# Differential attention inside a two-block network on one core: v panels three heads later, stages spaced by panels, the score bias added by TensorE

## The chip, the core and the metric

One core of a Trainium2 chip runs the whole forward pass of two blocks as one program. The metric is the device time of one execution in microseconds (us); the kernel before takes 2347.14 us (median of three runs, 2345.76 to 2347.51).

The core's engines run their own instruction queues in order and meet only at semaphores: TensorE (PE, matmuls and transposes into the eight banks of PSUM), VectorE (DVE), ScalarE (ACT), GpSimd (POOL) and SyncE (SP, which issues the weight loads).

## What is computed

Two blocks with thirteen phases: feed-forward layers, two hybrid mixers, one differential attention, one retention layer. The change is in the differential attention (phase `da`), 8 heads over 256 positions, head width 128 made of two halves of 64:

```python
def _diff_attention(xn, w_in, q_gain, k_gain, lam, subln, w_out, lam_init):
    q, k, v = jnp.split(xn @ w_in, 3, axis=-1)
    q = _rms(q.reshape(B, T, H, 2, Dh), q_gain) * (Dh ** -0.5)
    k = _rms(k.reshape(B, T, H, 2, Dh), k_gain)
    ...
    slopes = 2.0 ** (-8.0 * jnp.arange(1, H + 1, dtype=jnp.float32) / H)
    ...
        s = jnp.einsum('bhmqd,bhmkd->bhmqk', qb, k, preferred_element_type=jnp.float32)
        dist = (q_pos[:, None] - key_pos[None, :]).astype(jnp.float32)
        bias = jnp.where(dist >= 0, -slopes[:, None, None] * dist, -jnp.inf)
        p = jax.nn.softmax(s + bias[None, :, None], axis=-1)
        a = p[:, :, 0] - lmbda * p[:, :, 1]
        return jnp.einsum('bhqk,bhkd->bhqd', a.astype(v.dtype), v)
    ...
    o = _rms(o, subln) * (1.0 - lam_init)
    return o.reshape(B, T, H * 2 * Dh).astype(xn.dtype) @ w_out
```

## The kernel before

**Weights.** Every weight matrix is cut into panels of 128 output columns, [128, 1024] in float32. SP loads a panel into one of four slots of `raw` (`RING` is 4). ACT rounds it into `whi` (`act_split`, L318), DVE subtracts to get the rest `wlo` (`dve_split`, L325), and PE multiplies in three products per block of 128 rows (`products`, L308 to L310): 24 matmuls of 256 columns for one panel. The hi and lo parts of panel j+4 use the slot of panel j: ACT's split waits until PE has used panel j (`panel_used`), and DVE's waits for ACT's (`hi_ready`).

**The phase `da`** has 24 input panels, in the order q, k, v of head 0, q, k, v of head 1, and so on, then 8 output panels. A panel's result stands in bank 0 or 1, in turn, and DVE reads it out (`read_out`, L1342) times the row factor `R`; PE may start panel j when panel j-2 is read out (`a_evac`). Right behind each read-out, DVE makes the `wlo` of panel j+4.

**A head's stages** run one or more iterations of t behind its panels. With the line numbers of the profile: squares of q and k on ACT (`dsq`, L1041), their sums by a float32 matmul on PE (L683), the factor (`drq`, L402 and L404, ACT), q and k normed (`dn`, L1366, DVE), split into `dn_hi` (L1034, ACT) and `dn_lo` (L1389, DVE), scores (L723, PE, banks 6 and 7), bias (`dsc`, L1401), maxima (L1405, L1406) and their negation (L1408) on DVE, exponentials from `dsc` with their sums (`dp`, L1016, ACT), the weights `da_` (L1373 to L1383, DVE), their transposes (L733, PE), split into `dT_hi` (L1044, ACT) and `dT_lo` (L1411, DVE), v transposed (L701, PE) and split into `dv_hi` (L1025, ACT) and `dv_lo` (L1361, DVE), weighted values (L693, PE), a copy `do_` (L1357, DVE), its squares `dosq` (L1031, ACT), their sums (L740, PE), the factor `dro` (L402, L404, ACT), the normed output `don` (L1416, DVE), and its parts `dy_hi` (L1007, ACT) and `dy_lo` (L1347, DVE).

**What sets the order.** All of it is written out by hand, one loop over t for each engine; nothing is rescheduled. Each engine takes its queue strictly in that order, so an instruction that waits holds everything written behind it. When the input panels are through, PE fills in matmuls of the first four output panels (`out_tiles`) between the last heads' stages. The split of output panel 28 can't start before panel 24 has been used, so it comes after the last head.

## Time and profile before

| | us |
|---|---|
| median of three runs | 2347.14 |
| profiled execution, its own time | 2347.09 |
| its span on the core | 2345.3 |
| PE / DVE / ACT / POOL busy in the span | 2284.2 / 1484.6 / 1199.8 / 280.6 |
| phase `da`, first input panel to the next phase's first panel | 148.7 |
| granted TensorE clock over the span | 0.985 of full |

The page gives busy time by engine and by line. A matmul's record lasts longer than the spacing of two matmuls, so that a busy PE in the page is an engine with work in flight; where it loses time is read from its waits and from the timeline. The chain of waits follows the work that ended last back through the engines, and shows which engine's queue sets the pace of a stretch.

### The profile page before, as it was taken

Reading aid. Unit: us, or ns where it says so; the run is one execution under the profiler, and the core shown is the slowest. Engines: PE = TensorE matmul, PEld = TensorE weight load, DVE = VectorE, ACT = ScalarE, POOL = GpSimd, SP = SyncE. Lnnn points to the kernel's source line nnn. Section 1 sums busy time; section 2 is a strip of 40 time slices with the busy share of each in tenths; the row PEclk is TensorE's granted clock in tenths of the full one; section 3 lists DMA queues with packets and bytes.
Section 4 is the critical chain, followed back from the end, with each engine's and each line's share of the span. In section 5 each row is a group of like instructions: output and inputs, shape, how many; then the busy total and the mean of one; then the engine's idle time right before and its main releaser. Section 6 shows DMA issues by size and latency. Waiting matters only on the chain.

```text
span 2345.3 us, 48880 instructions
## 1 busy us (share of the span) xinstructions
PE 2284.2 (97%) x18478; PEld 2267.1 (97%) x18478; DVE 1484.6 (63%) x2284; ACT 1199.8 (51%) x1723; POOL 280.6 (12%) x328
## 2 busy tenths in 40 slices
PE   7999999999999999899998999889999999999999
PEld 7999999999999999899998999789999999999999
DVE  6655786665566468676656656866646655675663
ACT  5444675544444357654545545654535544464552
POOL 2001460300100125220010010020010010001000
PEclk9999999999999999899999999989999999999999
DMA  6555433555455553255554554325655555445563
GB/s 206 170 194 163 146 101 105 171 179 182 159 179 183 169 168 127 73 180 186 199 168 158 191 191 147 126 91 182 206 167 181 195 180 173 144 154 179 188 205 126
DMA packets 100881, 386.52 MB, mean 165 GB/s; under 512 B 11280, under 2 KB 13456, under 8 KB 100784
## 3 DMA queue, kind: packets, MB, share of 16 engines
q1 hardware_dynamic: 100128, 383.89, 49.8%
q8 instruction: 63, 1.03, 0.2%
q0 software_dynamic: 368, 1.20, 0.1%
q14 instruction: 34, 0.28, 0.0%
q10 hardware_dynamic: 288, 0.12, 0.0%
HBM read 384.11 MB, written 1.05 MB: 164 GB/s over the span
## 4 chain that ended last, share of the span: by engine, by line
PE 89%; DVE 6%; ACT 3%; issue 1%; POOL 0%; DMA 0%; ACTq 0%; POOLq 0%; DVEq 0%
PE bank L308 28%; PE bank L310 28%; PE bank L309 28%; DVE wlo L325 2%; ACT whi L318 1%; PE bank L540 1%; PE bank L669 1%; PE bank L570 1%; PE bank L795 0%; DVE qk L1237 0%; PE bank L583 0%; ACT dp L1016 0%; DVE dsc L1401 0%; DVE bank L1223 0%; PE bank L805 0%
## 5 line engine op out<-in xcount | busy, mean ns | idle before, releaser
L308 PE MATMUL bank<-u_hi,whi 128*128 128x256 f32 (+1 forms) x3968 | 1140.8, 287 | 20.2 <-DVE wlo L325 20.2
L310 PE MATMUL bank<-u_hi,wlo 128*128 128x256 f32 (+1 forms) x3968 | 1134.0, 286 | 0.0
L309 PE MATMUL bank<-u_lo,whi 128*128 128x256 f32 (+1 forms) x3968 | 1132.5, 285 | 0.0
L325 DVE TENSOR_TENSOR wlo<-raw,whi 128x1024 fp32r<-128x1024 f32 (+1 forms) x680 | 884.7, 1303 | 209.2 <-ACT whi L318 207.5
L318 ACT ACTIVATE whi<-raw 128x1024 fp32r<-128x1024 f32 (+1 forms) x680 | 746.5, 1111 | 286.6 <-PE bank L310 284.0
L308 PEld LDWEIGHTS bank<-u_hi,whi 128*128 128x128 f32 x3968 | 755.8, 190 | 21.5 <-DVE wlo L325 15.2
L310 PEld LDWEIGHTS bank<-u_hi,wlo 128*128 128x128 f32 x3968 | 755.8, 190 | 0.0
L309 PEld LDWEIGHTS bank<-u_lo,whi 128*128 128x128 f32 x3968 | 753.5, 190 | 0.7
L310 PE MATMUL bank<-hid_hi,wlo 128*128 128x256 f32 (+1 forms) x1408 | 400.6, 285 | 0.0
L308 PE MATMUL bank<-hid_hi,whi 128*128 128x256 f32 (+1 forms) x1408 | 399.4, 284 | 0.0
L309 PE MATMUL bank<-hid_lo,whi 128*128 128x256 f32 (+1 forms) x1408 | 398.1, 283 | 0.0
L1171 DVE TENSOR_TENSOR up<-bank,R 128x256 f32<-128x256 f32 (+1 forms) x176 | 75.7, 430 | 336.9 <-PE bank L310 336.9
L308 PEld LDWEIGHTS bank<-hid_hi,whi 128*128 128x128 f32 x1408 | 265.4, 188 | 0.0
L309 PEld LDWEIGHTS bank<-hid_lo,whi 128*128 128x128 f32 x1408 | 265.1, 188 | 0.0
L310 PEld LDWEIGHTS bank<-hid_hi,wlo 128*128 128x128 f32 x1408 | 264.7, 188 | 0.0
L339 ACT ACTIVATE u_hi<-h,gain 128x256 fp32r<-128x256 f32 (+1 forms) x88 | 44.6, 512 | 288.0 <-DVE h L1151 282.1
L365 POOL TENSOR_TENSOR ssq<-h 128x256 f32<-128x256 f32 (+1 forms) x12 | 10.4, 865 | 1353.0 <-DVE h L1151 1347.9
L861 ACT ACTIVATE sl<-gt 128x256 f32<-128x256 f32 (+1 forms) x160 | 67.7, 423 | 195.6 <-DVE gt L1169 195.5
L1151 DVE SCALAR_TENSOR_TENSOR h<-bank,h 128x256 f32<-128x256 f32 (+1 forms) x96 | 41.2, 429 | 194.2 <-PE bank L310 192.5
L865 ACT ACTIVATE hid_hi<-pr 128x256 f32 (+1 forms) x160 | 67.8, 424 | 154.7 <-DVE pr L1175 154.7
L1558 POOL TENSOR_TENSOR proj<-proj,tprod 128x272 f32<-128x272 f32 (+1 forms) x120 | 115.8, 989 | 88.0 <-ACT tprod L899 88.0
L370 POOL TENSOR_TENSOR sq<-h 128x256 f32<-128x256 f32 (+1 forms) x84 | 56.0, 666 | 366.5 <-DVE h L1151 364.5
(233 smaller groups left out, 2094.3 us busy)
## 6 DMA issues: line engine op xcount, KB each, us to landing
raw<-w SPq DMA_DIRECT2D x552, 512.0 KB, 3.3
raw<-w SPq DMA_DIRECT2D x128, 704.0 KB, 4.4
proj<-xT SPq DMA_DIRECT2D x2, 544.0 KB, 4.8
outT<-h SPq DMA_DIRECT2D x8, 128.0 KB, 4.6
consts<-cst POOLq DMA_DIRECT2D x1, 512.0 KB, 4.7
dist<-cst POOLq DMA_DIRECT2D x1, 192.0 KB, 2.7
rdist<-cst POOLq DMA_DIRECT2D x1, 192.0 KB, 2.7
sgain<-small POOLq DMA_DIRECT2D x1, 145.5 KB, 4.8
```

Of the source, the lines that this page charges most:

```text
L308: pe.matmul(out, w_h, x_hi, start=first, stop=False)
L309: pe.matmul(out, w_h, x_lo, start=False, stop=False)
L310: return pe.matmul(out, w_l, x_hi, start=False, stop=last)
L318: act.activation(whi[:, n % RING, 0:COLS[n]], raw[:, n % RING, 0:COLS[n]], ACT.Copy).then_inc(hi_ready, 1)
L325: dve.tensor_tensor(wlo[:, n % RING, 0:COLS[n]], raw[:, n % RING, 0:COLS[n]], whi[:, n % RING, 0:COLS[n]], ALU.subtract).then_inc(lo_ready, 1)
L339: act.activation(u_hi[:, f, win(y)], h[:, f, win(y)], ACT.Copy, scale=norm_gain(y, f)).then_inc(u_hi_ready, 1)
L370: pool.tensor_tensor(sq[:, win(y)], h[:, f, win(y)], h[:, f, win(y)], ALU.mult).then_inc(sq_done, 1)
L861: act.activation(sl[:, p, W], gt[:, p, W], ACT.Silu).then_inc(silu_done, 1)
L865: act.activation(hid_hi[:, f, W], pr[:, p, W], ACT.Copy).then_inc(hid_hi_ready, 1)
L1151: dve.scalar_tensor_tensor(out=h[:, f, W], in0=src, scalar=factor, in1=h[:, f, W], op0=ALU.mult, op1=ALU.add).then_inc(h_done, 1)
L1171: dve.tensor_tensor(up[:, p, W], bank[(g + 1) % 4][:, 0:N], R[:, W], ALU.mult).then_inc(a_evac, 1)
L1558: pool.tensor_tensor(acc, acc, tprod[:, (i - first) % TAP_RING, W2], ALU.add)\
```

## The change

- The input panels of `da` come in another order (`DA_PANELS`): iteration t brings q and k of head t and v of head t-3. The last three iterations' v panels stand behind q and k of head 7.
- A head's stages move: scores(t-2), transposes of the weights (t-3) and of v (t-4) stand behind the q panel, weighted values (t-4) behind the k panel, the q and k sums of head t and the output sums of head t-4 behind the v panel. ACT's and DVE's queues are reordered with them, and the tail is written out stage by stage on all three.
- The bias is added on PE: two matmuls of 384 columns for each head, `slope_r` (the identity times the slope) by `dist_r`. GpSimd makes both once (9 instructions). The 12 score matmuls alternate between the halves of the array instead of taking them one after the other.
- `dsc` is gone: DVE takes the maxima from banks 6 and 7, negated in the same instruction, and ACT's exponentials read the banks.
- The transposed weights have a bank of their own (5) and `dT_hi` and `dT_lo` two buffers; the output sums go to the second half of bank 3.

```diff
+V_LAG = 3
+DA_PANELS = [(part, t - (V_LAG if part == 2 else 0)) for t in range(DA_HEADS + V_LAG) for part in range(3)]
+DA_PANELS = [(part, hd) for part, hd in DA_PANELS if 0 <= hd < DA_HEADS]
...
+            dist_r = sb("dist_r", [128, 384], f32r, area)
+            slope_r = sb("slope_r", [128, DA_HEADS, 128], f32r, area)
...
-            dsc = sb("dsc", [128, 2, 384], f32, area)
...
+        bank = [ctx.enter_context(nc.psum_tensor(f"bank{i}", [128, 512], f32)) for i in range(6)]
+        pair67 = ctx.enter_context(nc.psum_tensor("bank67", [128, 2, 512], f32))
+        bank += [pair67[:, 0, :], pair67[:, 1, :]]
...
+                def qk_sums(hd):
+                    pe.wait_ge(d_sq_done, 2 * (hd + 1))
+                    pe.matmul(bank[4][:, :], mean_64, dsq[:, :, :].rearrange("p a t -> p (a t)"),
+                              start=True, stop=True).then_inc(d_qksum, 1)
+                def scores(hd):
+                    pe.wait_ge(d_n_ready, hd + 1)
+                    if hd == 0:
+                        pe.wait_ge(d_bias_ready, DA_HEADS + 1)
+                    else:
+                        pe.wait_ge(d_exps, 4 * hd)
+                    for i, (c0, w) in enumerate(((0, 128), (128, 256))):
+                        for n, (qq, kk) in enumerate(((dn_hi, dn_hi), (dn_hi, dn_lo), (dn_lo, dn_hi))):
+                            for m in range(2):
+                                rows = slice(64 * m, 64 * m + 64)
+                                pe.matmul(bank[6 + m][:, c0:c0 + w],
+                                          qq[rows, 0, 128 * i:128 * i + 128], kk[rows, 1, 0:w],
+                                          start=(i == 0 and n == 0), stop=False, skip_group_check=True)
+                    for m in range(2):
+                        mm = pe.matmul(bank[6 + m][:, 0:384], slope_r[:, hd, :], dist_r[:, :],
+                                       start=False, stop=True, skip_group_check=True)
+                    mm.then_inc(d_s_full, 1)
...
+                for t in range(DA_HEADS):
+                    in_panel2(y, DA_PANELS.index((0, t)))
                     if t == 0:
                         pe_norm(pe, y)
+                    if t >= 2:
+                        scores(t - 2)
                     if t >= 3:
+                        transpose_a(t - 3)
+                    if t >= 4:
+                        transpose_v(t - 4)
+                    if 1 <= t <= V_LAG:
+                        qk_sums(t - 1)
+                    in_panel2(y, DA_PANELS.index((1, t)))
+                    if t >= 4:
+                        weighted_values(t - 4)
+                    if t >= V_LAG:
+                        in_panel2(y, DA_PANELS.index((2, t - V_LAG)))
+                        qk_sums(t)
+                    if t >= 4:
+                        out_sums(t - 4)
+                in_panel2(y, DA_PANELS.index((2, 5)))
+                scores(6)
+                transpose_a(5)
+                transpose_v(4)
+                in_panel2(y, DA_PANELS.index((2, 6)))
+                weighted_values(4)
+                transpose_v(5)
+                in_panel2(y, DA_PANELS.index((2, 7)))
+                out_sums(4)
+                scores(7)
+                transpose_a(6)
+                transpose_v(6)
+                weighted_values(5)
+                out_tiles(0, 2, 0, 4)
+                out_sums(5)
+                transpose_v(7)
+                weighted_values(6)
+                out_tiles(2, RING, 0, 4)
+                out_sums(6)
+                transpose_a(7)
+                out_tiles(0, RING, 4, 6)
+                weighted_values(7)
+                out_tiles(0, RING, 6, 7)
+                out_sums(7)
...
+                def exps(hd):
+                    act.wait_ge(d_nmax, 2 * (hd + 1))
+                    for i, (c0, w) in enumerate(((0, 128), (128, 256))):
+                        for m in range(2):
+                            j = 2 * i + m
+                            act.activation(dp[:, m, c0:c0 + w], bank[6 + m][:, c0:c0 + w], ACT.Exp,
+                                           bias=dst[:, 4 + j:5 + j], accum_out=dst[:, 8 + j:9 + j])\
+                               .then_inc(d_exps, 1)
...
+                for t in range(DA_HEADS):
+                    if t >= 5:
+                        out_factor(t - 5)
+                    split(0, t)
                     if t >= 4:
+                        v_high(t - 4)
+                    if t >= 1:
+                        qk_factor(t - 1)
                     if t >= 3:
+                        weights_high(t - 3)
+                    if t >= 5:
+                        normed_hi(t - 5)
+                    if t >= 2:
+                        exps(t - 2)
+                    if t >= 1:
+                        qk_high(t - 1)
+                    split(1, t)
+                    if t >= 4:
+                        out_squares(t - 4)
+                    qk_squares(t)
+                    if t >= V_LAG:
+                        split(2, t - V_LAG)
...
+                def row_max(hd):
+                    dve.wait_ge(d_s_full, hd + 1)
+                    dve.tensor_reduce(dst[:, 4:6], pair67[:, :, 0:128], AX.X, ALU.max, negate=True).then_inc(d_nmax, 1)
+                    dve.tensor_reduce(dst[:, 6:8], pair67[:, :, 128:384], AX.X, ALU.max, negate=True).then_inc(d_nmax, 1)
...
-                            dve.scalar_tensor_tensor(out=dsc[:, m, :], in0=dist[:, :], scalar=-slopes[hd],
-                                                     in1=bank[6 + m][:, 0:384], op0=ALU.mult,
-                                                     op1=ALU.add).then_inc(d_sc_done, 1)
...
-                        dve.tensor_scalar(dst[:, 4:8], dst[:, 0:4], -1.0, None, ALU.mult).then_inc(d_nmax, 1)
...
+                for t in range(DA_HEADS):
+                    panel(0, t)
                     if t >= 4:
+                        v_low(t - 4)
+                    if t >= 2:
+                        row_max(t - 2)
+                    if t >= 5:
+                        normed(t - 5)
+                    if t >= 1:
+                        qk_normed(t - 1)
+                    panel(1, t)
                     if t >= 3:
+                        weights_low(t - 3)
+                    if t >= 4:
+                        out_copy(t - 4)
+                    if t >= 1:
+                        qk_low(t - 1)
+                    if t >= 5:
+                        normed_lo(t - 5)
+                    if t >= 2:
+                        weights(t - 2)
+                    if t >= V_LAG:
+                        panel(2, t - V_LAG)
...
+                    for hd in range(DA_HEADS):
+                        pool.tensor_scalar(slope_r[:, hd, :], ident, -2.0 ** (-8.0 * (hd + 1) / DA_HEADS), None,
+                                           ALU.mult).then_inc(d_bias_ready, 1)
+                    pool.wait_ge(table_loaded, 16)
+                    pool.tensor_copy(dist_r[:, :], dist[:, :]).then_inc(d_bias_ready, 1)
...
+            p8.append(w[[part * DA_HEADS + hd for part, hd in DA_PANELS]])
```

Lines of the changed kernel in the excerpts below: L317 to L319 panel matmuls, L327 `whi`, L334 `wlo`, L1445 read-out.

TensorE before, in iteration 5, from the output sums to the second panel (`d_osq` is the semaphore of `dosq`, `d_sq_done` of `dsq`):

```order
L740 MATMUL bank<-dosq,consts 128x256 [waits d_osq]
L308 MATMUL bank<-u_hi,whi 128x256 [waits a_evac,lo_ready]
...
L683 MATMUL bank<-dsq,consts 128x512 [waits d_sq_done]
L693 MATMUL bank<-dT_hi,dv_hi 128x256 [waits d_o_done,d_T_ready]
...
L701 MATMUL bank<-consts,dv 128x128 [waits a_evac]
...
L308 MATMUL bank<-u_hi,whi 128x256 [waits a_evac,lo_ready]
```

TensorE with the change, the same engine from the k panel's end in one iteration to the scores of the next:

```order
L737 MATMUL bank<-dT_hi,dv_hi 128x256 [waits d_ro_done,d_v_ready,d_T_ready]
...
L317 MATMUL bank<-u_hi,whi 128x256 [waits a_evac,lo_ready]
...
L687 MATMUL bank<-dsq,consts 128x512 [waits d_sq_done]
L745 MATMUL bank<-dosq,consts 128x256 [waits d_osq]
L317 MATMUL bank<-u_hi,whi 128x256 [waits a_evac,lo_ready]
...
L701 MATMUL bank<-dn_hi 128x128 [waits d_exps,d_n_ready]
```

The sums of q and k of head t now stand in the iteration that makes these panels, one panel behind k, where they stood a panel into the next iteration, two panels behind k.

ScalarE before, from the exponentials of one head to the squares of q and k:

```order
L1016 ACTIVATE dp,dst<-dsc,dst 128x256 x2
L1007 ACTIVATE dy_hi<-don 128x256 [waits d_on_done]
L318 ACTIVATE whi<-raw 128x1024 [waits panel_used,raw_loaded3]
L1025 ACTIVATE dv_hi<-bank 128x256 [waits d_vt_full]
L402 ACTIVATE drq<-bank,epsilons 128x512 [waits d_qksum]
L404 ACTIVATE drq<-drq 128x512 [waits d_rq_log]
L1031 ACTIVATE dosq<-do_ 128x256 [waits d_o_done]
L1034 ACTIVATE dn_hi<-dn 128x512 [waits d_n_done]
L318 ACTIVATE whi<-raw 128x1024 [waits panel_used,raw_loaded0]
L318 ACTIVATE whi<-raw 128x1024 [waits panel_used,raw_loaded1]
L1041 ACTIVATE dsq<-dqk 128x256 [waits a_evac]
```

ScalarE with the change, from the transposed weights to the squares of q and k in iteration 5:

```order
L1074 ACTIVATE dT_hi<-bank 128x384 [waits d_t_full]
L1057 ACTIVATE dy_hi<-don 128x256 [waits d_on_done]
L1081 ACTIVATE dp,dst<-bank,dst 128x128 [waits d_nmax]
L1081 ACTIVATE dp,dst<-bank,dst 128x128
L1081 ACTIVATE dp,dst<-bank,dst 128x256 x2
L1089 ACTIVATE dn_hi<-dn 128x512 [waits d_s_full,d_n_done]
L327 ACTIVATE whi<-raw 128x1024 [waits panel_used,raw_loaded1]
L1098 ACTIVATE dosq<-do_ 128x256 [waits d_o_done]
L1094 ACTIVATE dsq<-dqk 128x256 [waits a_evac]
L1094 ACTIVATE dsq<-dqk 128x256
L327 ACTIVATE whi<-raw 128x1024 [waits panel_used,raw_loaded2]
```

The squares `dosq` of another head's output moved to the place right ahead of `dsq`, and both stand behind the exponentials and the k panel's split.

VectorE with the change, in the same iteration, from the q panel's split to the copy `do_`:

```order
L334 TENSOR_TENSOR wlo<-raw,whi 128x1024 [waits hi_ready]
L1467 TENSOR_TENSOR dv_lo<-bank,dv_hi 128x256 [waits d_v_hi]
L1472 TENSOR_REDUCE dst<-bank 128x2 [waits d_s_full]
L1473 TENSOR_REDUCE dst<-bank 128x2
L1462 SCALAR_TENSOR_TENSOR don<-do_,lam,dro 128x256 [waits d_y_ready,d_ro_done]
L1478 SCALAR_TENSOR_TENSOR dn<-dqk,lam,drq 128x256 [waits d_rq_done]
L1478 SCALAR_TENSOR_TENSOR dn<-dqk,sgain,drq 128x256
L1445 TENSOR_TENSOR dqk<-bank,R 128x256 [waits panel_used]
L334 TENSOR_TENSOR wlo<-raw,whi 128x1024 [waits hi_ready]
L1506 TENSOR_TENSOR dT_lo<-bank,dT_hi 128x384 [waits d_T_hi]
L1514 COPY do_<-bank 128x256 [waits d_on_done,d_osq,d_av_full]
```

The maxima moved from behind two panels' read-outs and splits to between the q and the k panel; the copy `do_` stands behind the k panel's split.

## Rows read from the trace of the kernel before

**Rows 1.** The page, busy us of each engine, share of the span, instructions

```profile
PE 2284.2 (97%) x18478; PEld 2267.1 (97%) x18478; DVE 1484.6 (63%) x2284; ACT 1199.8 (51%) x1723; POOL 280.6 (12%) x328
```

**Rows 2.** Busy time in stretches of `da`: its iterations 0 to 3, one later, tail

```profile
core 0: us, PE busy (x) PEld busy (x) DVE busy (x) ACT busy (x) POOL busy (x), PEclk, DMA share, GB/s
1420.60:1479.60 59.00, 56.07 (x454) 52.17 (x452) 45.54 (x89) 39.78 (x79) 2.05 (x3) 1.00 0.43 140
1479.60:1493.10 13.50, 12.35 (x102) 11.37 (x100) 11.36 (x26) 9.58 (x23) 0.00 (x0) 1.00 0.37 117
...
1520.10:1551.90 31.80, 22.83 (x132) 20.02 (x130) 16.22 (x41) 13.42 (x38) 0.00 (x0) 0.77 0.11 34
```

**Rows 3.** Chain of waits in one iteration of `da`: start us, us, what

```profile
1480.66 0.94 DVE dsc L1401 x2
...
1482.04 0.60 DVE dst L1406
...
1482.88 0.87 ACT dp L1016 x4
...
1484.74 0.31 ACT dy_hi L1007
1485.05 0.96 ACT whi L318
...
1486.03 1.22 DVE wlo L325
...
1487.59 0.33 DVE do_ L1357
```

**Rows 4.** Timeline of DVE and ACT in that iteration: start us, us, what

```profile
1482.75 0.55 DVE L1411 TENSOR_TENSOR dT_lo<-bank,dT_hi 128x384 fp32r<-128x384 f32 x1
1483.22 0.47 DVE L1416 SCALAR_TENSOR_TENSOR don<-do_,lam,dro 128x256 f32<-128x256 f32 x1
...
1478.10 0.72 ACT L1041 ACTIVATE dsq<-dqk 128x256 f32<-128x256 f32 x2
...
1487.96 0.42 ACT L1031 ACTIVATE dosq<-do_ 128x256 f32<-128x256 f32 x1 [0.46 <-DVE do_ L1357]
1489.08 0.63 ACT L1034 ACTIVATE dn_hi<-dn 128x512 fp32r<-128x512 f32 x1 [0.70 <-DVE dn L1366]
```

**Rows 5.** Groups by line and form in that iteration: busy us, mean ns

```profile
L1007 ACT ACTIVATE dy_hi<-don 128x256 fp32r<-128x256 f32 x1 | 0.4, 400 | 0.0
...
L1025 ACT ACTIVATE dv_hi<-bank 128x256 fp32r<-128x256 f32 x1 | 0.4, 361 | 0.0
```

**Rows 6.** Timeline: PE from sums to transposes, a panel's end, a wait before scores

```profile
1432.39 1.02 PE L683 MATMUL bank<-dsq,consts 128*128 128x512 f32 x2
1433.25 0.38 PE L701 MATMUL bank<-consts,dv 128*128 128x128 f32 x2
...
1439.03 0.28 PE L310 MATMUL bank<-u_hi,wlo 128*128 128x256 f32 x1
...
1439.40 1.06 ACT L318 ACTIVATE whi<-raw 128x1024 fp32r<-128x1024 f32 x1 [1.58 <-PE bank L310]
...
1451.41 0.33 PE L723 MATMUL bank<-dn_hi 64*128 64x128 f32 x1 [1.15 <-DVE dn_lo L1389]
```

**Rows 7.** PE's waits over the whole run: us in total, times, longest

```profile
PE bank L540 <- ACT at_hi L974: 9.1, 5, 2.3
...
PE bank L693 <- DVE dT_lo L1411: 4.6, 3, 2.6
PE bank L669 <- DVE dy_lo L1347: 4.2, 2, 2.4
```

**Rows 8.** Timeline of PE: two of its waits, idle us in brackets

```profile
992.52 0.39 PE L308 MATMUL bank<-qk,whi 128*128 128x256 f32 x1 [1.56 <-DVE proj L1312]
...
1523.87 0.58 PE L693 MATMUL bank<-dT_hi,dv_hi 128*128 128x256 f32 x1 [2.56 <-DVE dT_lo L1411]
```

**Rows 9.** Busy time right behind one of the mixer's waits, columns as in rows 2

```profile
352.90:359.60 6.70, 6.70 (x31) 6.68 (x31) 0.78 (x2) 2.03 (x4) 1.73 (x2) 0.50 0.01 2
```

More of the change, by code:

```diff
@@ new lines, in weighted_values @@
+                def weighted_values(hd):
+                    pe.wait_ge(d_T_ready, hd + 1)
+                    pe.wait_ge(d_v_ready, hd + 1)
+                    if hd >= 1:
+                        pe.wait_ge(d_ro_done, hd)
+                    for i, (c0, t0) in enumerate(((0, 0), (256, 128))):
+                        for n, (vv, aa) in enumerate(((dv_hi, dT_hi), (dv_hi, dT_lo), (dv_lo, dT_hi))):
+                            mm = pe.matmul(bank[3][:, t0:SEQ], vv[:, hd % 2, 128 * i:128 * i + 128],
+                                           aa[:, hd % 2, c0:c0 + SEQ - t0], start=(i == 0 and n == 0),
+                                           stop=(i == 1 and n == 2), skip_group_check=True)
+                    mm.then_inc(d_av_full, 1)
@@ L685, in da @@
                     if t >= 3:
-                        hd = t - 3
-                        pe.wait_ge(d_T_ready, hd + 1)
-                        if hd >= 1:
-                            pe.wait_ge(d_o_done, hd)
-                        for i, (c0, t0) in enumerate(((0, 0), (256, 128))):
-                            for n, (vv, aa) in enumerate(((dv_hi, dT_hi), (dv_hi, dT_lo), (dv_lo, dT_hi))):
-                                mm = pe.matmul(bank[3][:, t0:SEQ], vv[:, hd % 2, 128 * i:128 * i + 128],
-                                               aa[:, c0:c0 + SEQ - t0], start=(i == 0 and n == 0),
-                                               stop=(i == 1 and n == 2), skip_group_check=True)
@@ new lines, in qk_high, with qk_squares @@
+                def qk_high(hd):
+                    act.wait_ge(d_n_done, 2 * (hd + 1))
+                    if hd >= 1:
+                        act.wait_ge(d_s_full, hd)
+                    act.activation(dn_hi[:, :, :], dn[:, :, :], ACT.Copy).then_inc(d_n_hi, 1)
+                def qk_squares(hd):
+                    act.wait_ge(a_evac, A + DA_PANELS.index((1, hd)) + 1)
+                    for i in range(2):
+                        act.activation(dsq[:, i, :], dqk[:, hd % 2, i, :], ACT.Square).then_inc(d_sq_done, 1)
@@ new lines, in panel, with normed @@
+                def panel(part, hd):
+                    if part == 2 and hd >= 1:
+                        dve.wait_ge(d_vt_full, hd)
+                    read_out(DA_PANELS.index((part, hd)), dv[:, :] if part == 2 else dqk[:, hd % 2, part, :])
+                def normed(hd):
+                    dve.wait_ge(d_ro_done, hd + 1)
+                    if hd >= 1:
+                        dve.wait_ge(d_y_ready, hd)
+                    dve.scalar_tensor_tensor(out=don[:, :], in0=do_[:, :], scalar=sub_gain, in1=dro[:, :],
+                                             op0=ALU.mult, op1=ALU.mult).then_inc(d_on_done, 1)
@@ new lines, in da @@
+                qk_normed(7)
+                normed(3)
+                panel(2, 5)
+                v_low(4)
+                row_max(6)
+                weights_low(5)
+                qk_low(7)
+                normed_lo(3)
+                out_copy(4)
+                weights(6)
+                panel(2, 6)
+                v_low(5)
+                normed(4)
+                row_max(7)
+                weights_low(6)
+                normed_lo(4)
+                panel(2, 7)
+                v_low(6)
```

273 lines of the change are left out of this document (121 added, 152 removed).

## The prediction

> **What bounds the kernel now.** I read the page first. It calls TensorE 97% busy [rows 1], but this counts records that overlap. The table by stretches comes next: in each later iteration of phase `da` (13.5 us) DVE is busy 11.4, ACT 9.6 and PE 12.4, at full clock; the tail of 31.8 us has PE busy 22.8 and a granted clock of 0.77 [rows 2]. In such an iteration PE waits 1.15 us ahead of the scores, for DVE [rows 6]. So PE's own work is 13.5 - 1.2 = 12.3 us per head, and something else makes 13.5.
>
> The chain of waits says what [rows 3]. It runs on DVE all the time but for one piece: maxima, then ACT's four exponentials (from 1482.88 to the next instruction at 1484.74), `dy_hi` 0.31, the split `whi` 0.96, and back to DVE's `wlo` 1.22. DVE needs that split before it may go on. A loop over two in-order queues sets the pace: 10.3 us of DVE and 3.2 of ACT, 13.5 in all.
>
> **The change, part by part.**
>
> *DVE's work per head.* `dsc` goes (0.94 [rows 3]), and the negation with it, about 0.2. The maxima stay at 0.34 + 0.60 [rows 3]. That they read PSUM costs nothing by the rows, and ACT gains: it takes `dv_hi` out of PSUM in 361 ns and `dy_hi` out of SBUF in 400 [rows 5], so four exponentials save 0.1 to 0.2. The Trainium skill (Perfetto Trace Analysis, Optimizing Scalar/DVE Operations) gives DVE a higher fixed cost on PSUM than on SBUF, some 65 ns more, and ACT a lower one, some 42 ns less; ACT's rows agree. By the page the pair is worth 2 x 0.065 - 4 x 0.042, nothing, per head.
>
> *PE's work per head.* Two bias matmuls of 384 columns. The trace has none; between the panel's spacing of 0.119 for 256 columns (2.86 a panel) and 0.43 for one pass of a 512-column float32 sum (half of 1432.39 to 1433.25 [rows 6]) I take 0.17 each, near the first, 0.33 a head, range 0.24 to 0.86. The alternating scores give some back, 0 to 0.4. PE stays at about 12.2 a head; this is not on the chain below.
>
> *GpSimd's nine instructions* have fifteen us until the first scores. They cost nothing; without that cover a few us, once.
>
> *The order.* This is the main term. I follow the new queues through iteration t (5 to 7), with the lengths from the rows, each as start to next start:
> 1. PE's q panel, start to last matmul 2.8, then 0.37 until ACT's split starts (1439.03 to 1439.40 [rows 6]): 3.2.
> 2. `whi` of the q slot 1.0 to 1.1, DVE's `wlo` 1.15, `dv_lo` 0.33: 2.5 [rows 3].
> 3. Maxima 0.94, `don` 0.47 [rows 3, 4], which now stands right behind them: 1.4.
> 4. ACT: `dy_hi` 0.31, exponentials 1.7, `dn_hi` 0.54 [rows 3, 4]: 2.6.
> 5. `whi` of the k slot 1.1, `wlo` 1.15: 2.25.
> 6. DVE's `dT_lo` 0.47 and copy `do_` 0.42 + 0.03 [rows 3, 4]: 0.9.
> 7. ACT's `dosq` 0.33, then `dsq` twice 0.72 [rows 4]: 1.1.
> 8. PE's q and k sums 0.82 [rows 6], output sums 0.25: 1.1. Behind them is the q panel of t+1.
>
> Sum 15.05; I take 15.0. Each link is either the next instruction of an in-order queue or a semaphore. The loop before held one split pair with the exponentials between; this one holds two splits, the exponentials, the copy with two squares and one PE panel. PE arrives at the sums 12.2 us after it left them, so it **waits 2.8 us per head there**, where it waited 1.2 before the scores. Queued behind the waiting sums are the output sums and the q panel, and the whole chain waits for that panel. Iteration 4 has no `don` and `dy_hi` yet, 14.2.
>
> The same way for the rest. *Iterations 0 to 3* make only 9 of the 24 panels: 9 x 2.86 + four q and k sums 3.3 + two sets of scores 2.4 + the norm and one transpose 0.6 = 32.0, and 1.7 of waits for DVE's `dn_lo` and weights: 33.7. *Iterations 4 to 7*: 14.2 + 3 x 15.0 = 59.2. *Tail*, three v panels among it: from the v panel of head 5, DVE and ACT alternate through q/k norm (6.6), maxima to exponentials of head 6 (2.9), exponentials to `dn_lo` (2.9), weights and a read-out (4.4), maxima to `dT_hi` and `dy_hi` (3.9), a read-out, split, `dv_lo`, copy and square (3.1): 23.8. Then PE work of 11.0 to the last sums, the last normalisation 2.8, and 12 matmuls 1.4: 39.0. Sum 33.7 + 59.2 + 39.0 = 131.9.
>
> Before it is 59.0 + 3 x 13.5 + 31.8 + 1.4 = 132.7 [rows 2], of which about 5 are due to the half clock in the tail. From here on both kernels have the same four output panels. So at full clock the change comes out 0.8 us shorter than the row of before, and 4 longer than before would be at full clock.
>
> *The clock* decides the rest. In the trace every PE wait of 1.8 us or more stands beside a stretch at 0.5: the four of about 2.2 in the mixers, those of 2.56 and 1.91 for `dT_lo`, those of 1.80 and 2.44 for `dy_lo` [rows 7, 8]. The one of 1.56 [rows 8] and the 1.15s do not. Behind one of 2.2 the clock is at 0.5, its 1.2 GHz level, for 6.7 us, and 31 matmuls take the time that 56 would at 0.119 [rows 9]: 3.0 us lost. The new waits are 2.0 (iteration 4) and 2.8 (5, 6, 7), and what follows each is on the chain: 1.1 of sums and a panel, 4 us of PE work, so the loss lands in full. Bounds 0 to 4 x 3.0; I take three of four, 9.0. The tail still has two long waits (ahead of output sums 3.4, of the last matmuls 2.6): 2.5. Together 11.5.
>
> Forecast: 2347.1 - 0.8 + 11.5 = **2357.8 us**. The profiled run's 2347.09 is its span and 1.8, and equals the median.
>
> **Rivals.**
> - *The clock stays up.* Waits of 2.8 every 15 us leave long work between. Then only the tail's 2.5 is left: 2347.1 - 0.8 + 2.5 = 2348.8, no change that can be told. For it: in iterations of 15 us with 12.2 of matmuls PE is busier than in the mixers. Against: eight of eight in the rows. The Trainium skill (TensorE: Matmul & The Clock Gate, Why this matters for your kernels) warns only of idle gaps longer than any of these, which is this rival's case; the rows speak against that rule. Chance 0.10.
> - *Some waits only*: one or two at 3.0, 2351.8 to 2355. Chance 0.17.
> - *The other side, faster.* The chain decides only if ACT reaches `dsq` later than PE reaches the sums. If its links overlap by more than 2.8 us, PE's 12.2 sets the pace: 4 x 2.8 less, no half clock in the middle: 2348.8 - 10.4 = 2338.4. For it: DVE's and ACT's work per head is down to 10.2 and 9.1. Against: the same reading gives 13.5 for before, which is the measured period. Chance 0.13.
> - *The change misses its cover further*: all four waits, a third one in the tail, the maxima slower on PSUM across two banks: 2362 to 2368. Chance 0.10.
> - The forecast's own case, 2355 to 2362: 0.50.
>
> **How the numbers follow.** The range reaches from 2346, which takes in the rival with the clock up, to 2366; what is left out is the faster case and the end of the slow one, under 0.2. A measurement of this kernel can tell 0.2%, 4.7 us, from no change. Slower by more (over 2351.8): 0.50 + 0.10 + 0.13 of the third case = 0.73. Within: 0.10 + 0.04 = 0.14. Faster (under 2342.4): 0.13.
>
> **What the profile of the changed kernel would show.** Iterations 5 to 7 of `da` with a period of 15 or, with half clock, 18 us; PE's longest wait in the phase ahead of the q and k sums, put down to ACT's `dsq`, 2.0 to 2.9 each, and none of 1 us ahead of the scores; a granted clock under 1 in the middle of the phase, where it is 1.00 now; a chain of waits that goes panel, `whi`, `wlo`, maxima, `don`, `dy_hi`, exponentials, `whi`, `wlo`, copy, squares, sums. Wrong: a period near 12.3 and PE unbroken; or a period of 15 at full clock, which would make the clock step wrong; or scores with bias over 2 us.

## The result

The changed kernel takes **2355.26 us** (median of 7, 2354.32 to 2357.07), the kernel before it, measured beside it, 2347.85 (7, 2345.76 to 2349.14). The ratio is 1.0031, with a 95% interval of 1.002 to 1.0042: slower by 0.3%. The forecast was 2357.8 in a range of 2346 to 2366, with 0.73 on slower. The profiled execution took 2355.55 us, its span is 2353.8.

One number is used for all kernels below. The phases ahead of `da` are the same code in all of them, but in the profiled executions they end anywhere from 1417.4 to 1421.2, so I compare the time **from the first matmul of `da` to the end of the span**: 924.7 before (first matmul at 1420.64 of 2345.3) and 933.4 after (1420.42 of 2353.8). The change costs 8.7 us there. Each of these numbers is from one profiled execution, and a stretch of 3.4 us at half clock (a granted clock of 0.50) more or less moves it by up to 1.7.

### The profile page after: what moved, and what is told of

Its sections match the earlier page's. It is cut to its first block, busy times and chain, and to the rows that moved or that the text cites. A ratio compares the mean times of both kernels' runs of the same rounds, so it can differ in the third digit from the quotient of the medians.

```text
span 2353.8 us, 48939 instructions
## 1 busy us (share of the span) xinstructions
PE 2287.5 (97%) x18494; PEld 2269.5 (96%) x18494; DVE 1476.9 (63%) x2260; ACT 1197.7 (51%) x1723; POOL 287.2 (12%) x337
## 4 chain that ended last, share of the span: by engine, by line
PE 89%; DVE 5%; ACT 4%; issue 1%; POOL 0%; DMA 0%; ACTq 0%; DVEq 0%; POOLq 0%
PE bank L317 28%; PE bank L319 28%; PE bank L318 28%; DVE wlo L334 2%; ACT whi L327 1%; PE bank L549 1%; PE bank L579 1%; ACT dp L1081 0%; PE bank L845 0%; DVE qk L1341 0%; PE bank L592 0%; PE bank L678 0%; DVE u_lo L355 0%; PE bank L687 0%; DVE bank L1327 0%
## 5 line engine op out<-in xcount | busy, mean ns | idle before, releaser
L317 PE MATMUL bank<-u_hi,whi 128*128 128x256 f32 (+1 forms) x3968 | 1146.2, 289 | 20.2 <-DVE wlo L334 20.1
L319 PE MATMUL bank<-u_hi,wlo 128*128 128x256 f32 (+1 forms) x3968 | 1136.9, 287 | 0.0
L334 DVE TENSOR_TENSOR wlo<-raw,whi 128x1024 fp32r<-128x1024 f32 (+1 forms) x680 | 886.2, 1305 | 210.5 <-ACT whi L327 208.6
L327 ACT ACTIVATE whi<-raw 128x1024 fp32r<-128x1024 f32 (+1 forms) x680 | 747.4, 1112 | 296.6 <-PE bank L319 294.4
L317 PEld LDWEIGHTS bank<-u_hi,whi 128*128 128x128 f32 x3968 | 758.8, 191 | 22.5 <-DVE wlo L334 15.0
L319 PEld LDWEIGHTS bank<-u_hi,wlo 128*128 128x128 f32 x3968 | 758.5, 191 | 0.0
L319 PE MATMUL bank<-hid_hi,wlo 128*128 128x256 f32 (+1 forms) x1408 | 401.1, 285 | 0.0
L317 PE MATMUL bank<-hid_hi,whi 128*128 128x256 f32 (+1 forms) x1408 | 399.9, 284 | 0.0
L317 PEld LDWEIGHTS bank<-hid_hi,whi 128*128 128x128 f32 x1408 | 265.7, 189 | 0.0
L319 PEld LDWEIGHTS bank<-hid_hi,wlo 128*128 128x128 f32 x1408 | 265.1, 188 | 0.0
```

The costliest lines, as they stand in the source:

```text
L317: pe.matmul(out, w_h, x_hi, start=first, stop=False)
L319: return pe.matmul(out, w_l, x_hi, start=False, stop=last)
L327: act.activation(whi[:, n % RING, 0:COLS[n]], raw[:, n % RING, 0:COLS[n]], ACT.Copy).then_inc(hi_ready, 1)
L334: dve.tensor_tensor(wlo[:, n % RING, 0:COLS[n]], raw[:, n % RING, 0:COLS[n]], whi[:, n % RING, 0:COLS[n]], ALU.subtract).then_inc(lo_ready, 1)
```

## The profile after

The page's busy line of the changed kernel answers to [rows 1]:

```profile
PE 2287.5 (97%) x18494; PEld 2269.5 (96%) x18494; DVE 1476.9 (63%) x2260; ACT 1197.7 (51%) x1723; POOL 287.2 (12%) x337
```

DVE lost 24 instructions and 7.7 us, TensorE has 16 matmuls and 3.3 us, GpSimd 9 instructions and 6.6 us more. This line alone does not say where the 8.7 us come from.

Busy time in stretches of `da` of the changed kernel, columns as in [rows 2]: iterations 0 to 3; iteration 6; then two pieces, one behind the third of four waits and one behind the fourth; and, from another answer, the tail, from its first v panel to the last output matmul:

```profile
1420.42:1454.15 33.73, 32.55 (x260) 29.75 (x258) 23.35 (x39) 24.63 (x49) 9.21 (x12) 1.00 0.47 150
1485.95:1502.68 16.73, 14.16 (x103) 13.05 (x102) 10.38 (x23) 9.39 (x22) 0.00 (x0) 0.90 0.30 93
...
1502.90:1506.20 3.30, 3.30 (x17) 3.30 (x16) 1.46 (x2) 0.89 (x2) 0.00 (x0) 0.50 0.17 43
1519.60:1523.00 3.40, 3.40 (x34) 3.24 (x32) 1.56 (x3) 1.12 (x3) 0.00 (x0) 1.00 0.17 37
```
```profile
1519.48:1562.85 43.37, 34.11 (x247) 31.20 (x245) 22.39 (x51) 20.12 (x51) 0.61 (x1) 0.90 0.15 49
```

Read the second row against the 13.50 of [rows 2]: DVE is busy a full microsecond less, and the iteration is 3.2 us longer. 2.57 of the 16.73 are idle PE, and the granted clock is 0.90, where it was 1.00.

PE's waits in `da` after (us in total, times, longest), to be read beside [rows 7]:

```profile
PE bank L687 <- ACT dsq L1094: 9.7, 4, 2.6
PE bank L745 <- ACT dosq L1098: 4.1, 2, 3.0
PE bank L678 <- DVE dy_lo L1450: 2.4, 1, 2.4
...
PE bank L701 <- DVE dn_lo L1484: 1.1, 2, 0.7
```

The wait ahead of the scores (1.15 an iteration in [rows 6]) is gone; in its place PE waits four times, 9.7 us together, ahead of the q and k sums (line 687), for ACT's squares. The timeline of PE shows the first of them and the third:

```profile
1467.82 0.70 PE L687 MATMUL bank<-dsq,consts 128*128 128x512 f32 x1 [1.95 <-ACT dsq L1094]
...
1501.48 1.13 PE L687 MATMUL bank<-dsq,consts 128*128 128x512 f32 x2 [2.57 <-ACT dsq L1094]
1502.44 0.66 PE L745 MATMUL bank<-dosq,consts 128*128 128x256 f32 x2
1502.68 0.63 PE L317 MATMUL bank<-u_hi,whi 128*128 128x256 f32 x1
```

The chain of waits through iteration 6 (start us, us, what), to be read beside [rows 3]. The panel's matmuls between the first row and `whi` are left out:

```profile
1486.51 0.21 PE bank L317
...
1490.70 1.07 ACT whi L327
...
1491.79 1.23 DVE wlo L334
...
1493.38 0.41 DVE dst L1472
1493.79 0.60 DVE dst L1473
1494.39 0.40 DVE don L1462
...
1494.82 0.05 ACT dy_hi L1057
...
1496.84 0.52 ACT dn_hi L1089
1497.36 0.95 ACT whi L327
...
1499.48 0.55 DVE dT_lo L1506
1500.03 0.34 DVE do_ L1514
...
1500.40 0.03 ACT dosq L1098
...
1500.72 0.71 ACT dsq L1094 x2
...
1501.48 1.13 PE bank L687 x2
1502.61 0.49 PE bank L745 x2
```

These are the eight links of the prediction in their order. The lengths, start to next start: panel 4.75 (1485.95 to 1490.70; predicted 3.2), `whi`, `wlo`, `dv_lo` 2.68 (2.5), maxima and `don` 1.44 (1.4), `dy_hi`, exponentials, `dn_hi` 2.54 (2.6), the second split pair 2.12 (2.25), `dT_lo` and copy 0.92 (0.9), squares 1.08 (1.1), sums 1.20 (1.1). Together 16.73. Only the panel is far off, by 1.55, and it is off because many of its matmuls stand 0.21 apart, at half clock; the other seven are within 0.2 each.

## The experiments

Before a chip ran any of them two theories stood. **The loop**: PE waits because the q and k sums close a loop over three in-order queues, 15 us long, and the clock adds to it. **PE's own work**: the two bias matmuls, or something else on PE, make the time. e5 to e8 were thought out after the first four had run. The table gives the time, its ratio to the kernel before with the 95% interval, and the time from the first matmul of `da` to the end; the last is from one profiled execution. The kernel before was timed again beside each set: 2347.9 belongs to e1 to e4, 2346.4 to e5 to e8, and the changed kernel has the 2347.85 of the result. Each ratio is to the one beside it.

| kernel | us | ratio | from `da` |
|---|---|---|---|
| before | 2347.9 and 2346.4 (two sets) | 1 | 924.7 |
| changed | 2355.3 | 1.0031 (1.0020 to 1.0042) | 933.4 |
| e1: old order, bias on PE | 2336.1 | 0.9955 (0.9941 to 0.9968) | 913.5 |
| e2: changed, sums later | 2340.9 | 0.9972 (0.9963 to 0.9982) | 917.4 |
| e3: changed, matmuls in the wait | 2351.4 | 1.0016 (1.0007 to 1.0025) | 927.6 |
| e4: changed, bias on DVE | 2370.5 | 1.0096 (1.0080 to 1.0111) | 948.3 |
| e5: e1, scores alternating | 2334.3 | 0.9950 (0.9937 to 0.9964) | 911.6 |
| e6: changed, `dsq` first | 2344.9 | 0.9994 (0.9985 to 1.0004) | 922.7 |
| e7: changed, matmuls behind the wait | 2361.7 | 1.0067 (1.0052 to 1.0082) | 939.6 |
| e8: e5, sums earlier in the tail | 2331.6 | 0.9939 (0.9926 to 0.9953) | 910.4 |

### e1: the bias on TensorE alone, in the old order

> The order of panels and stages is that of the kernel before; only the bias goes to TensorE, the maxima and exponentials read PSUM. Loop theory: the 13.5 us loop of before loses dsc (0.94), the negation (0.2) and some of the exponentials (0.1), so that TensorE's own 12.3 us per head sets the pace; no new wait over 1.8 us in the iterations, granted clock 1.00 there. Median 2337 to 2341, against 2347.9 for before. Rival (the bias on TensorE or reading PSUM is what made the change slower): 2348 to 2356.

The kernel before, with nothing of the new order. In PE's `scores`, in ACT's exponentials and in DVE's maxima:

```diff
+                        for m in range(2):
+                            mm = pe.matmul(bank[6 + m][:, 0:384], slope_r[:, hd, :], dist_r[:, :],
+                                           start=False, stop=True, skip_group_check=True)
...
-                                act.activation(dp[:, m, c0:c0 + w], dsc[:, m, c0:c0 + w], ACT.Exp,
+                                act.activation(dp[:, m, c0:c0 + w], bank[6 + m][:, c0:c0 + w], ACT.Exp,
...
-                            dve.scalar_tensor_tensor(out=dsc[:, m, :], in0=dist[:, :], scalar=-slopes[hd],
...
+                        dve.tensor_reduce(dst[:, 4:6], pair67[:, :, 0:128], AX.X, ALU.max, negate=True).then_inc(d_nmax, 1)
+                        dve.tensor_reduce(dst[:, 6:8], pair67[:, :, 128:384], AX.X, ALU.max, negate=True).then_inc(d_nmax, 1)
```

It is 0.45% faster than before, just under the lower end of what I expected. One iteration of e1, same columns as above, and its PE timeline from the scores on:

```profile
1464.70:1477.40 12.70, 12.70 (x103) 11.86 (x102) 10.47 (x22) 9.49 (x23) 0.00 (x0) 1.00 0.38 129
```
```profile
1472.20 0.33 PE L728 MATMUL bank<-dn_hi 64*128 64x128 f32 x1
...
1473.37 0.62 PE L733 MATMUL bank<-dist_r,slope_r 128*128 128x384 f32 x2
1473.83 0.49 PE L741 MATMUL bank<-consts,da_ 128*128 128x128 f32 x3
```

PE is busy for all of 12.70: the DVE-ACT loop of 13.5 is now shorter than PE's own work, and there is no wait in an iteration. The scores with bias take 1.63 us (1472.20 to 1473.83), where those of before take 1.17, so the two bias matmuls cost 0.46, not 0.33, and inside the range of 0.24 to 0.86. The change holds a part that gains 11 us; whatever loses is in the order. Only 4.3 of the 11 lie ahead of the output sums of iteration 7 (99.2 us from the first matmul of `da` before, 94.9 in e1). The other 6.8 lie behind, where before has stretches of 6.8, 3.4 and 13.7 us at half clock and e1 has none.

### e5: and the scores alternate

> The order of the kernel before, with the bias on TensorE and maxima and exponentials from PSUM, as e1, and in addition the twelve score matmuls alternate between the two halves. In e1 the period of an iteration was 12.7 us and PE waited for nothing of 0.9 us or more in it, so PE sets the pace there. In the kernel before and in e1 the twelve take some 1.17 us, in the changed kernel and in e4 some 0.86. Theory (the pace is PE's own work): the period falls by the 0.3 us that the alternation saves, to 12.4, and eight heads give 2.4 us: 2333 to 2335. Rival (DVE-ACT loop is just as long as PE's work by now, so that a shorter PE only waits): period stays 12.7, 2336, and PE gets waits of 0.3 us ahead of the scores.

```diff
-                        for m in range(2):
-                            rows = slice(64 * m, 64 * m + 64)
-                            for i, (c0, w) in enumerate(((0, 128), (128, 256))):
-                                for n, (qq, kk) in enumerate(((dn_hi, dn_hi), (dn_hi, dn_lo), (dn_lo, dn_hi))):
+                        for i, (c0, w) in enumerate(((0, 128), (128, 256))):
+                            for n, (qq, kk) in enumerate(((dn_hi, dn_hi), (dn_hi, dn_lo), (dn_lo, dn_hi))):
+                                for m in range(2):
+                                    rows = slice(64 * m, 64 * m + 64)
```

The same rows of e5:

```profile
1467.30:1479.75 12.45, 12.45 (x103) 11.61 (x102) 10.38 (x22) 9.48 (x23) 0.00 (x0) 1.00 0.39 128
```
```profile
1474.82 0.33 PE L728 MATMUL bank<-dn_hi 64*128 64x128 f32 x2
...
1475.70 0.62 PE L733 MATMUL bank<-dist_r,slope_r 128*128 128x384 f32 x2
1476.16 0.49 PE L741 MATMUL bank<-consts,da_ 128*128 128x128 f32 x3
```

The block is 1.34 (1474.82 to 1476.16) and the period 12.4; PE stays unbroken, as the theory wanted and the rival did not. From `da` on that is 2.0 us less. The two ratios overlap, so it is the traces that show this gain, not the times alone; neither trace has a stretch at half clock in the phase. Against e5 the order of the changed kernel costs 933.4 - 911.6 = **21.8 us**, of which some 8.5 are half clock by the estimates of the part on the prediction (4.8 in the iterations, 3.7 in the tail).

### e2: the sums later in the new order

> The change, with one edit: the sums of q and k and of the outputs stand behind the next q panel on TensorE instead of ahead of it (and the output factor behind the q panel's split on ScalarE). Loop theory: the panel no longer waits for the squares, the loop of 15 us is cut, the period falls to 12.3 us, the three waits of 2.6 us and their stretches at half clock go: 2341 to 2345. Rival (the three heads' delay of v, or the work itself, costs the time): 2353 to 2357.

```diff
                     if t == 0:
                         pe_norm(pe, y)
+                    if t >= 5:
+                        out_sums(t - 5)
+                    if t >= 4:
+                        qk_sums(t - 1)
                     if t >= 2:
                         scores(t - 2)
...
                         in_panel2(y, DA_PANELS.index((2, t - V_LAG)))
-                        qk_sums(t)
-                    if t >= 4:
-                        out_sums(t - 4)
```

ACT's `out_factor` moves behind `split(0, t)` to match. The q panel of t+1 is no longer queued behind the waiting sums. One iteration of e2:

```profile
1469.60:1482.00 12.40, 12.40 (x103) 11.42 (x102) 9.27 (x20) 8.72 (x22) 0.00 (x0) 1.00 0.39 117
```

The period is 12.4 for 16.7, with no wait and no half clock in it; from `da` on it takes 16.0 us less than the changed kernel, some of it because its tail has 6.8 us at half clock where that one's has 13.7. Its median of 2340.9 is just under the 2341 to 2345 expected. What it still loses to e5, 5.8 us, must be outside these iterations, which are as long as e5's. Over the whole phase (140.8 us, e5's is 134.9) PE is idle 2.5 us more and busy 3.4 us more. Two stretches of 3.4 us at half clock in e2's tail, where e5 has none, account for about 3.0 of the busy time (half of the 3.2 and 2.9 that PE is busy in them).

### e6: one step of ACT turned round

> The changed kernel with one step of ACT's order turned round: the squares of q and k (dsq) stand ahead of the square of the output (dosq), so they don't wait for DVE's dT_lo and copy do_. Theory (the loop of eight links that the prediction gives is what sets 15 us): without the 0.9 us of dT_lo and copy and the 0.33 of dosq ahead of dsq the period of iterations 5 to 7 falls from 15.2 to about 13.5 to 14; what is left of the wait is at the output sums, about 1 us for dosq, and the waits at the q and k sums are under 0.5. Waits that short bring no stretch at a clock of 0.5 in the iterations. Together 5.8 plus 3 x 1.5: 2345 to 2350. Rival (PE's wait is owed to something outside the loop, so that it only moves behind the q and k sums in full): period stays 15, 2355.

```diff
+                    qk_squares(t)
                     if t >= 4:
                         out_squares(t - 4)
-                    qk_squares(t)
```

One iteration of e6, and its wait for a square (us in total, times, longest):

```profile
1478.40:1492.20 13.80, 12.96 (x101) 11.57 (x101) 10.47 (x23) 9.29 (x22) 0.00 (x0) 1.00 0.35 114
```
```profile
PE bank L745 <- ACT dosq L1098: 6.9, 6, 3.0
```

Two calls in another order give 10.7 us back (933.4 to 922.7), and with 0.9994 the kernel can't be told from before. The period is 13.8 where the links said 13.5 to 14; the waits ahead of `dsq` are gone from the list, what is left is for `dosq`, under a microsecond an iteration, and no stretch of the iterations is at half clock. The copy `do_` and `dT_lo` were links of the loop: with `dsq` ahead of them they are links only of the shorter loop through `dosq`.

### e3 and e7: the same matmuls in the wait and behind it

> The change plus ten needless matmuls of 384 columns (1.6 us) on TensorE ahead of each wait for the squares from iteration 4 on. They shorten the wait, not the chain. Clock theory: with waits of 1 us the clock stays at 1.00 in the iterations, and 3 x 1.5 us come back though TensorE does 6.4 us more work: 2350 to 2352. Rival (the clock costs nothing here, the loop alone does): 2355, unchanged. Rival (TensorE's work is the bound): 2360 or more.

> The changed kernel with ten needless matmuls of 384 columns (1.6 us) ahead of each q panel of the iterations 5 to 7 and ahead of the v panel of head 5, that is on the loop, behind the wait instead of in it; the output is not changed by them. It is the counterpart of e3, in which the same matmuls stood in the wait and cost nothing. Theory (the q panel is a link of the loop): PE's own work per head grows by 1.6 and the loop by the same, so the waits ahead of the sums stay as they are, 2.6 each, and the time grows by 4 x 1.6: 2361 to 2362. Rival (PE's work behind the sums has slack, as it would if the wait were for a transfer or another engine's own pace): waits shrink by 1.6, time as e3's, 2351 to 2355.

Both add needless matmuls that leave the output alone; in e3 they write the bank of the sums ahead of them, in e7 the bank of the panel that follows.

```diff
+                    for _ in range(count):
+                        pe.matmul(bank[4][:, 0:384], slope_r[:, 0, :], dist_r[:, :], start=True, stop=True)
...
                         in_panel2(y, DA_PANELS.index((2, t - V_LAG)))
+                        if t >= 4:
+                            filler(t, 10)
                         qk_sums(t)
```
```diff
+                    if t >= 5:
+                        filler(DA_PANELS.index((0, t)), 10)
...
+                filler(DA_PANELS.index((2, 5)), 10)
                 in_panel2(y, DA_PANELS.index((2, 5)))
```

The waits for `dsq` in e3, then in e7:

```profile
PE bank L687 <- ACT dsq L1102: 2.6, 4, 0.8
```
```profile
PE bank L687 <- ACT dsq L1103: 9.7, 4, 2.6
```

An iteration of e3, then one of e7:

```profile
1483.80:1499.10 15.30, 14.44 (x112) 13.29 (x112) 10.51 (x23) 9.43 (x23) 0.00 (x0) 1.00 0.31 97
```
```profile
1485.80:1504.40 18.60, 16.02 (x111) 14.30 (x111) 10.47 (x23) 9.39 (x23) 0.00 (x0) 0.91 0.25 82
```

In e7 the waits stay as they were and the turns, from sums to sums, are 18.56, 18.59 and 17.02 us against the changed kernel's 16.84, 16.82 and 16.80: the ten matmuls lengthen a turn by 1.7 to 1.8, about their own length, once it is counted that only the first two have a stretch at half clock. The q panel is on the loop. That e7's time meets the forecast so well is in part luck, since the stretch that is missing there is made up in its tail, where one is 10.2 us long. In e3 the ten take the place of waiting (9.7 to 2.6 us), and the kernel gets *faster* by doing more, 5.8 us from `da` on, 3.9 in the medians. Its periods are 15.26, 15.26 and 15.24 at full clock, which is 4.7 us less in three turns; the other 1.1 lie in the tail, where e3 has 6.8 us at half clock and the changed kernel 13.7. So the **loop itself is 15.25 us, and the half clock adds 1.6 to a turn**, three times.

### e4: the new order, the bias on DVE

> The change with the bias, its negation and the exponentials' source put back as they were (on VectorE, from SBUF), in the new order. Loop theory: they stand on the loop of 15 us with 1.3 us per head, so iterations 4 to 7 get 1.3 longer each and the tail 2 to 3: 2361 to 2366. Rival (the bias on TensorE costs time): below 2354.

`scores` without its two bias matmuls, the exponentials out of `dsc`, and in `row_max` what was there before:

```diff
-                    dve.tensor_reduce(dst[:, 4:6], pair67[:, :, 0:128], AX.X, ALU.max, negate=True).then_inc(d_nmax, 1)
+                        dve.scalar_tensor_tensor(out=dsc[:, m, :], in0=dist[:, :], scalar=-2.0 ** (-8.0 * (hd + 1) / DA_HEADS),
+                                                 in1=bank[6 + m][:, 0:384], op0=ALU.mult,
+                                                 op1=ALU.add).then_inc(d_sc_done, 1)
...
+                    dve.tensor_scalar(dst[:, 4:8], dst[:, 0:4], -1.0, None, ALU.mult).then_inc(d_nmax, 1)
```

PE's waits for the squares, and one iteration:

```profile
PE bank L686 <- ACT dsq L1087: 16.4, 4, 4.3
```
```profile
1508.00:1526.20 18.20, 13.92 (x100) 12.24 (x100) 11.56 (x26) 9.53 (x23) 0.00 (x0) 0.88 0.29 93
```

The longest wait is 1.7 longer than in the changed kernel. I put this down to about 1.2 that DVE and ACT do more in the loop and the 0.46 of bias that PE no longer does; the two were not tried apart. I had expected 2361 to 2366 and it took 2370.5. Of the 14.9 us to the changed kernel 6.2 lie between the sums of iterations 3 and 7 (15.3, 18.2, 19.2 and 18.2 for 14.2, 16.8, 16.8 and 16.8), where I had expected 5.2; 2.3 lie in the iterations ahead, which I had not priced, and 6.4 behind, in the tail, which I had put at 2 to 3. Behind the last wait for `dsq` 26.3 us are at half clock in e4 and 13.7 in the changed kernel, so much of the tail's 6.4 may be the clock. In the new order, then, the bias on TensorE is worth 14.9 us, in the old one 11.2, both with what the clock adds to them. The order alone, without the part that pays for some of it, costs 23.6, alternating scores included.

### e8: the tail of e5

> e5 with one more step in the tail of the phase: the output sums of head 6 stand on PE ahead of an output-tile group that needs nothing of them, so that the last heads' normalisation starts while PE works on that group. Theory (in the tail the chain runs through the last outputs' normalisation, PE has slack there): up to 2.5 us earlier, 2331 to 2333. Rival (the group that moves back is itself on the path): as e5, within 1 us.

```diff
-                    if t == DA_HEADS + 1:
-                        out_tiles(0, RING, 5, 6)
...
+                    if t == DA_HEADS + 1:
+                        out_tiles(0, RING, 5, 6)
```

The output sums stand between the two places. The medians fell by 2.7 us, the traces from `da` on by 1.2 only; the two ratios overlap, and I count 1.2. Why not the 2.5 of the theory: the waits of 1.80 and 2.44 of e5 became 0.38 and 2.44, and the last twelve matmuls, alike in both but for the clock, first in e5, then in e8:

```profile
1539.20:1542.30 3.10, 1.68 (x12) 1.48 (x12) 1.72 (x2) 2.39 (x3) 0.61 (x1) 1.00 0.00 0
```
```profile
1536.05:1539.40 3.35, 2.93 (x12) 2.64 (x12) 1.52 (x3) 1.93 (x3) 0.84 (x1) 0.50 0.00 0
```

Both stand behind the same wait of 2.44 for `dy_lo`; in e8 half clock takes 1.25 us of the gain back. It is the fastest of all: 0.9939 of the kernel before (0.9926 to 0.9953), and 23.0 us less than the changed kernel from `da` on.

## The prediction, step by step

**What bounds the kernel before: right.** With 1.2 us taken off DVE and ACT, e1's iteration becomes PE's own work, 12.7, or 12.4 with alternating scores. The 12.3 that I read as 13.5 less the waits was that work, with the bias to be added. The larger part of what e1 won lies in the tail, where before has 23.9 us at half clock; the prediction put about 5 us of that tail down to it.

**DVE's and ACT's savings: right, nearly.** Per iteration DVE is busy 10.38 (predicted 10.2), ACT 9.39; the 9.1 that the prediction gives for ACT does not follow from its own rows, 9.58 less 0.2. The changed kernel's maxima and exponentials by line and form (busy us, mean ns):

```profile
L1081 ACT ACTIVATE dp<-bank,dst 128x256 f32<-128x256 f32 x2 | 0.9, 474 | 0.0
...
L1473 DVE TENSOR_REDUCE dst<-bank 128x2 f32<-128x512 f32 x1 | 0.7, 680 | 0.0
...
L1472 DVE TENSOR_REDUCE dst<-bank 128x2 f32<-128x256 f32 x1 | 0.4, 414 | 0.0
```

and the kernel before's, out of SBUF:

```profile
L1016 ACT ACTIVATE dp<-dsc,dst 128x256 f32<-128x256 f32 x2 | 1.0, 493 | 0.0
...
L1406 DVE TENSOR_REDUCE dst<-dsc 128x2 f32<-128x512 f32 x1 | 0.7, 675 | 0.0
L1405 DVE TENSOR_REDUCE dst<-dsc 128x2 f32<-128x256 f32 x1 | 0.4, 420 | 0.0
```

DVE reads PSUM at SBUF's price (675 to 680, 420 to 414). ACT gains 19 ns at 256 columns and 40 at 128 (394 to 354); the four exponentials go from 1.77 us, start to next start, to 1.58. The Trainium skill (Perfetto Trace Analysis, Optimizing Scalar/DVE Operations) has DVE some 65 ns dearer on PSUM, which these rows don't show, and ACT some 42 cheaper, with which the 128 columns agree and the 256 don't. The page gives engine-busy times and these rows are profiled durations, so they test its figures only in part.

**PE's work: close.** Bias 0.46 a head for 0.33, alternation 0.29 back; 12.4 a head in e2 and e5 for 12.2. GpSimd's nine instructions cost nothing that the waits show: PE's first wait for scores is for `dn_lo`.

**The loop: right.** The eight links are the chain of the changed kernel, e6 and e2 shorten it where they should, e7 lengthens it. Full-clock length 15.25 for 15.0; waits 1.95 and three of 2.57 for 2.0 and 2.8. With half clock a turn is 16.8, between the 15 and the 18 that the prediction named. From sums to sums iteration 4 took 14.24 for 14.2; from q panel to q panel 15.2, since the output sums are new in it and what follows its wait is at half clock. So iterations 4 to 7 are 60.5 without the half clock, for 59.2.

**The term that was mis-sized: the half clock.** I took 9.0 us from three of four waits at 3.0. Three of four it was; the rows gave no reason for three, so the count is luck, and e7 with the same waits had two. But the stretches at 0.50 lasted 3.4 us (1502.85 to 1506.26 for the third) and not the 6.7 of [rows 9]. Some 17 matmuls ran in such a stretch where 28 would have at 0.119, which is 1.4 us; e3 prices a turn at 1.6. That is 4.8, not 9.0. The trace of before held this length too, behind its wait of 1.91 for `dT_lo`:

```profile
1537.30:1540.60 3.30, 3.30 (x18) 3.30 (x17) 2.27 (x8) 0.63 (x2) 0.00 (x0) 0.50 0.00 0
```

Nor does the wait alone set it: ahead of `da`, where the code is the same in all kernels, the first wait of 2.8 in a mixer goes with a stretch of 6.8 in the traces of before, the changed kernel and e5, and with one of 3.4 in e1 and e8. One row behind one wait was too little to price four others. Iterations 0 to 3 took 33.7 as predicted, iterations 4 to 7 took 65.3 for 68.2.

**The tail: the path right, the clock low.** From the v panel of head 5 to the output sums of head 4 I worked out 23.8; the trace has 1519.48 to 1543.29, 23.8. From there to the last matmul's end at 1562.85 it took 19.6 for 15.2 + 2.5. Two stretches at 0.50 lie in it, the end from 1560.87 on and this one:

```profile
1543.90:1550.60 6.70, 5.33 (x25) 4.95 (x24) 2.24 (x6) 1.89 (x5) 0.00 (x0) 0.50 0.17 65
```

Half of its busy 5.3 us and half of the last 2.0 is an estimated 3.7, for my 2.5; 0.7 more I can't place. The tail's two long waits were 3.04 ahead of the output sums (predicted 3.4) and 2.44 ahead of the last matmuls (2.6).

**The base: 1.5 us short.** I let the last twelve matmuls of before take 1.4; they ran at half clock, as the timeline of before shows, and took 2.9.

```profile
1551.90 0.58 PE L669 MATMUL bank<-dy_hi,whi 128*128 128x256 f32 x1 [2.44 <-DVE dy_lo L1347]
...
1554.42 0.41 PE L669 MATMUL bank<-dy_hi,wlo 128*128 128x256 f32 x1
```

So the predicted difference of 10.7 (143.4 less 132.7) and the measured 8.2 (33.7 + 65.3 + 43.4 = 142.4, less 134.2; the other 0.5 of the 8.7 us lie behind these matmuls) differ by -4.2 (half clock in the iterations), +1.3 (links), +1.9 (tail) and -1.5 (base), together -2.5. Errors of 8.9 us cancel to 2.5, and that is luck. The forecast missed the median by 2.5 as well, but from the medians side by side the change costs 7.4, so there the difference was off by 3.3, and the kernel before came out 0.7 higher than in the forecast.

**The claim on the clock: too strong.** "Every wait of 1.8 us or more" held in the rows of before. It does not hold after: the fourth wait of 2.57 is followed by 34 matmuls in 3.40 at 1.00 (the last row of the first group of stretches above), and in e1 and e5 waits of 1.80 and 2.44 in the tail bring nothing. What the prediction argued against the Trainium skill (TensorE: Matmul & The Clock Gate, Why this matters for your kernels) stands: gaps shorter than those it warns of are followed by half clock, three times in four here. What decides between two waits of the same length these runs don't tell; e5 and e8 differ in what stood ahead of theirs, and the changed kernel with matmuls behind its waits (e7) had two of four. It **stays open**.

**The rivals.** "Clock stays up" would have been 2348.8: out. "Some waits only", with one or two of them at 3.0, had the number of waits wrong, but the 4.8 us measured lie between its 3 and 6, and the time at the upper end of its 2351.8 to 2355: by size the result is nearer to it than to the forecast of 2357.8. "Misses its cover further" (2362 to 2368) is out. "Faster, because the links overlap" failed, since they don't: every link of the chain waits for the one ahead. (Its 2338.4 takes 10.4 us off, the waits of 2.0 and three times 2.8, and not the 4 x 2.8 that it names.)

## What to carry to other kernels

Work taken off an engine paid in both orders here, because the loop of each runs through that engine. Before taking a new order, walk one iteration through all in-order queues, semaphore by semaphore, from an instruction back to itself; a sum longer than the busiest engine's work is the new period, and an instruction queued behind another that waits (here a panel behind a small sum, or `dsq` behind `dosq`) is the first thing to turn round. Try a change's parts apart: here the bias and the alternation together were worth 13 us and the order cost 22. And read the granted clock in the tail of the kernel before: a change can win or lose there more than in the loop that it is aimed at.

## What the runs showed of the hardware

- Two groups of K = 64 matmuls on the two halves of the rows, written by turns and not one group after the other, shorten twelve of them with the step to the next from 1.17 to 0.88 us (1472.20 to 1473.37 in e1, 1474.82 to 1475.70 in e5). The rows merge them in pairs with the length of one, 0.33.
- More matmuls can make a kernel faster: e3's 40 needless ones, 6.6 us of PE work in time that was waited anyway, brought 3.9 us in the medians.
- The half clock that follows a wait was 3.4 us long in the iterations of the changed kernel and 6.8 in its tail. Ahead of `da` the same wait of 2.8 us in the same code goes with 6.8 us in some kernels' traces and 3.4 in others'.
